# Output projection of a feed-forward block in two-by-two blocks: the pair groups as three, four and four in place of four, four and three

## What is computed

```python
def conv_ffn(x, w_in, conv_w, conv_b, w_out):        # x: 1 x 1024 x 1024
    h = causal_depthwise_conv(x @ w_in, conv_w, conv_b)  # w_in: 1024 x 5632, three taps along the tokens
    val, gate = jnp.split(h, 2, axis=-1)
    return (jax.nn.silu(gate) * val) @ w_out         # w_out: 2816 x 1024
...
x = x + conv_ffn(rms_norm(x, norm_ffn_g), ...)
```

## Time and profile before

| | |
|---|---|
| three executions | 2439.64, 2433.68, 2439.77 us; median 2439.64 |
| the profiled execution | 2434.73 us; its span 2432.9 us |
| TensorE matmul busy | 2294.0 us, 94% of the span |
| VectorE, ScalarE, GpSimd busy | 1598.2, 1293.5, 1076.4 us |
| mean granted TensorE clock | 0.982 |
| first matmul of P0, start | 1916.46 us |
| units 1 to 13 end | 2429.8 us, then the last addition and the last transfer out |

### The profile page before, as it was taken

How to read it: one execution, slowest core, us unless ns; L and a number is a source line. 1 busy time by engine, 2 the same in 40 slices (tenths; PEclk the granted TensorE clock), 3 DMA queues, 4 the chain that set the end, 5 groups by cost and what they waited for, 6 DMA issues and landing times. The chain is left out here.

```text
span 2432.9 us, 35474 instructions
## 1 busy us (share of the span) xinstructions
PE 2294.0 (94%) x11778; PEld 1940.5 (80%) x11778; DVE 1598.2 (66%) x3055; ACT 1293.5 (53%) x2966; POOL 1076.4 (44%) x1125
## 2 busy tenths in 40 slices
PE   7999999999999999999999998989988999997999
PEld 6788778878888878888888887877767788875787
DVE  7444666667885333356656665587978688897975
ACT  6444566666775434456656665555544454553432
POOL 5554322311245642321222223577766656564643
PEclk9999999999999999999999999999989999998999
DMA  6322101111243332222223224422343623345732
GB/s 220 113 71 66 40 23 31 31 33 49 64 135 100 94 128 70 91 74 83 83 85 92 85 83 144 137 86 85 96 160 109 186 87 102 102 150 187 226 108 82
DMA packets 332164, 242.73 MB, mean 100 GB/s; under 512 B 66256, under 2 KB 286672, under 8 KB 331472
## 3 DMA queue, kind: packets, MB, share of 16 engines
q1 hardware_dynamic: 331984, 240.47, 32.4%
HBM read 196.64 MB, written 43.78 MB: 99 GB/s over the span
## 5 line engine op out<-in xcount | busy, mean ns | idle before, releaser
L2758 POOL TENSOR_TENSOR WS<-WR,WS 128x256 fp32r<-128x256 f32 x647 | 505.4, 801 | 982.0 <-ACT WS L2110 979.5
L1869 PE MATMUL PS<-HT,WS 128*128 128x512 f32 x1488 | 605.2, 407 | 32.5 <-POOL WS L2758 9.4
L1871 PE MATMUL PS<-HT,WS 128*128 128x512 f32 x1488 | 586.3, 394 | 0.0
L1870 PE MATMUL PS<-HT,WS 128*128 128x512 f32 x1488 | 584.3, 393 | 0.0
L1869 PEld LDWEIGHTS PS<-HT,WS 128*128 128x128 f32 x1488 | 282.8, 190 | 94.6 <-issue 26.0
L1871 PEld LDWEIGHTS PS<-HT,WS 128*128 128x128 f32 x1488 | 282.0, 190 | 62.2
L1870 PEld LDWEIGHTS PS<-HT,WS 128*128 128x128 f32 x1488 | 283.1, 190 | 52.2
L2110 ACT ACTIVATE PT<-PS 128x512 fp32r<-128x512 f32 x352 | 186.3, 529 | 222.3 <-PE PS L1982 221.9
L2110 ACT ACTIVATE WS<-WR 128x256 fp32r<-128x256 f32 x662 | 247.2, 410 | 105.0 <-PE PS L1871 57.0
L2350 DVE TENSOR_TENSOR PT<-PS,PT 128x512 fp32r<-128x512 f32 x352 | 210.8, 609 | 66.9 <-ACT PT L2110 64.5
L2015 PE MATMUL PS<-PT,QKV 128*128 128x256 f32 (+1 forms) x1248 | 208.1, 288 | 3.4 <-DVE YB L2529 2.3
(11 more groups left out here) (297 smaller groups left out, 4922.6 us busy)
## 6 DMA issues: line engine op xcount, KB each, us to landing
WR<-in_w_in_odd SPq DMA_DIRECT2D x106, 256.0 KB, 2.9
EO<-in_grid SPq DMA_DIRECT2D x48, 384.0 KB, 3.1
WR<-in_ffn_in SPq DMA_DIRECT2D x64, 256.0 KB, 2.9
WR<-in_w_in_even SPq DMA_DIRECT2D x100, 128.0 KB, 2.5
WR<-in_w_out_odd SPq DMA_DIRECT2D x48, 256.0 KB, 2.8
yd<-PY SPq DMA_DIRECT2D x44, 256.0 KB, 3.2
WR<-ud SPq DMA_DIRECT2D x39, 256.0 KB, 3.1
EO<-in_ffn_in SPq DMA_DIRECT2D x35, 256.0 KB, 3.0
```

The lines of the kernel that those rows point to most:

```text
L1869: e.matmul(out, wh, rh, start=start, stop=False)
L1870: e.matmul(out, wh, rl, start=False, stop=False)
L1871: return e.matmul(out, wl, rh, start=False, stop=stop)
L2758: e.tensor_tensor(ws(i, 1, n), RAW[raw_slot(u)][:, o:o + n], f32(ws(i, 0, n)), ALU.subtract).then_inc(s_wlop.sem, 1)
```

## The change

```diff
-GROUPS = ((0, 4), (8, 4), (16, 3))
+GROUPS = ((0, 3), (6, 4), (14, 4))
```

## The result

| | before | after |
|---|---|---|
| median | 2436.28 us (20 runs, 2433.68 to 2440.96) | 2443.41 us (20 runs, 2437.31 to 2447.67) |
| ratio | | 1.0027 [1.0020, 1.0034] |
| profiled execution, span | 2434.73, 2432.9 us | 2438.33, 2436.5 us |
| TensorE, VectorE, GpSimd busy | 2294.0, 1598.2, 1076.4 us | 2293.9, 1599.0, 1078.6 us |

What follows compares the result with a forecast made beforehand. VectorE's work at the first group's entry, then two chained reloads, and VectorE nearly from P103 to P126 were taken as bounds. Terms -12 - 5.5 + 0.8 + 1.4 + 19.04 = +3.7 us gave 2443 us, range 2430 to 2453.

Steps and rivals of the forecast that it cites:

- up to P99's addition: Entry of the first group: fewer low parts, narrower weight sums and shorter VectorE waits bring this addition 12 us earlier.
- P103 to P126: Units 8 and 9: VectorE becomes the bound, the stretch takes 60.7 us, 5.5 less than 66.25.
- unit 10: Starts with VectorE a little further behind; its loss of 1.38 us grows to about 2.2, +0.8.
- unit 12: Loses 1.4 us because unit 11 now prepares four pairs rather than three.
- I count for each what VectorE lost to one GpSimd instruction: Entry: five of seven removed low parts ran while VectorE worked, each giving back 1.1 us, 5.5 us together.
- unit 7 near 39: Sign that the forecast holds: unit 7 takes near 39 us, where it took 47.96.
- no stop ahead of P96 over 2 us: Sign at the entry: TensorE's 6.08 us stop ahead of P96 shrinks to about 1, none over 2.
- The chain of the reloads: Entry: from reload 0's issue to P99's addition, two reload latencies one behind the other, kept at 13.3 us.
- P102's stop: Entry: TensorE still stops ahead of P102 about as long as before, 12 us.
- Rival 1: Entry healed, VectorE's lateness all gone: P99's addition 24.7 us earlier, total -9.0, 2431 us; chance 0.15.
- Rival 2: Unit 9 stuck: P103 to P126 takes its 66 us again, total +9.2, 2449 us; chance 0.2.
- Rival 3: Load ring and SyncE's strict order bind: only 6 us up to P99, total +9.7, 2449 us; chance 0.1.

Runs made afterwards that it cites:

- a1: Kernel before (groups 4,4,3) with the seven GpSimd low parts of the first group's fourth pair left out: 2431.64 us, ratio 0.9977.
- a3: Changed kernel (3,4,4) with the 21 VectorE low parts of the second group left out: 2436.31 us, ratio 1.0002 to the kernel before.
- a4: Changed kernel (3,4,4) with all 28 loads of the second group's operands left out: 2439.0 us, ratio 1.0011 to the kernel before.
- b1: Kernel before (4,4,3) with reloads of X ahead of the same product's u loads, reload 2 right behind reload 0: 2428.91 us, ratio 0.9962.
- b2: Changed kernel (3,4,4) with reloads of X ahead of u loads, reload 2 right behind reload 0: 2434.96 us, ratio 0.9991 to the kernel before.
- b3: Kernel before with groups of 4, 3 and 4 pairs in place of 4, 4, 3: 2443.27 us, ratio 1.0027.
- a2: Kernel before (4,4,3) with the seven loads of the first group's fourth pair left out: 2435.79 us, ratio 0.9996.
- b4: Kernel before (4,4,3) with the first group's fourth-pair low parts on VectorE in place of GpSimd: 2433.49 us, ratio 0.9983.
- c1: Kernel before (4,4,3) with the reloads first and the first group's fourth low parts on VectorE: 2426.21 us, ratio 0.9958.
- c2: Kernel before (4,4,3) with the reloads first and every group's fourth low parts on VectorE: 2425.05 us, ratio 0.9948.
- c3: Changed kernel (3,4,4) with the reloads first and all low parts of u on VectorE: 2432.95 us, ratio 0.9983 to the kernel before.

## Why the prediction was right or wrong

The forecast of 2443.0 against a median of 2443.41 is closer than its steps deserve: it was built on a median of before that is 3.4 us above the one of 20 runs, and the sum was 3.4 too small (+3.7 against +7.1). By its own steps, in the stage:

| term | predicted | measured |
|---|---|---|
| up to P99's addition | -12 | -9.5 |
| P103 to P126 | -5.5 | -4.7 |
| unit 10 | +0.8 | -1.4 |
| unit 12 | +1.4 | +1.4 |
| units 12 and 13 longer | +19.0 | +19.0 |
| sum | +3.7 | +4.8 |

- **What bounds it** was right: VectorE's work at the entry, the reload chain, and VectorE in P103 to P126. a1 and a3 show the first and the last; the chain's cause was seen only in part, below.
- **Up to P99's addition** is the term that failed most. It was made of 8 us of VectorE's busy time and 4 of its waits, with the chain unchanged. Measured: busy 59.35 to 54.97, so 4.4; the waits for tiles of u 5.86 to 3.22, so 2.6; the chain 2.4 shorter. The step "I count for each what VectorE lost to one GpSimd instruction" has the right price (a1: 1.1 each) and the wrong conclusion, that what is left of GpSimd's work would not come to lie on VectorE's: three instructions did, for 3.3 us. The sums were priced from one slow row (1.77), while the four took 5.86 together; they gave back 3.65 and not 1.1, and the low parts of u 0.4. For the same reason "unit 7 near 39" and "no stop ahead of P96 over 2 us" failed: 42.50 and 2.55. That the three moved is read from the traces, with a1, where they stayed, as the nearest control; no run moved them alone.
- **The chain of the reloads** was described as standing behind loads that wait for "those very splits", and then kept at 13.3. I didn't ask which loads stand there: the last two or three are those of the second group, which nobody needs yet. The 2.4 by which the chain did shrink came mostly from transfers that landed sooner, which the step didn't foresee. a4, b1 and b2 show that 6 to 7 us of the entry were there in both kernels.
- **P102's stop** as long as before (12.03), P103's shorter than the 4 foretold (2.86).
- **P103 to P126**: VectorE is 58.77 us busy (58.7 foretold) of 61.49 (60.7), 95.6%. The mechanism is right (a3), the idle time kept is 2.7 rather than 2.
- **Unit 10** was to fall further behind and instead lost nothing. What VectorE is behind is now paid inside unit 9, at P123 and P124 (a stop of 4.07), ahead of the boundary. The mechanism was right, its place wrong, and the term had the wrong sign.
- **The rivals.** Rival 1 didn't come about: P99's addition is 9.5 us earlier, not 24.7. Rival 2 foretold 66 us for P103 to P126 and has 61.5; as a general mechanism (a light unit can't use its short products) it holds for 7 of 9.5 us (b3). Rival 3 foretold 6 us up to P99 and the entry gave 9.5; the number of loads is out by a2, but the strict order of SyncE's list, which it names too, held up the reloads by some 6 us in both kernels (a4, b1, b2).
- **Still open:** the stage gives +4.8, the medians +7.1. The profiled executions differ by +3.6, of which -1.3 is the part ahead of unit 7. The trace of after is of one of its fastest executions, 5.1 under the median, that of before 1.6 under its own, so what the slower executions lose stands in neither. Over the five kernels with 3,4,4 the ratio of times exceeds what the stage shows by -0.7 to 3.2 us, so it's no steady term, and I can't place it.

## What to carry to other kernels

Moving the light part of a job to the front helps only if the engine that is late there is freed by the lightening: here matmuls went away and VectorE's additions, splits and taps stayed, so 20.5 us in units 12 and 13 were given up for 15.6 in units 7 to 10. Before resizing stages, read what stands *ahead* of the late transfer on its queue; moving two reloads past loads that could not start anyway gave 0.9962, while neither other table of groups gained anything. And when an instruction on a neighbouring engine is taken away, look where the rest of that engine's list will fall: what ran in an idle gap may come to lie where it hurts as much.

## What the hardware showed unexpectedly

A subtraction on GpSimd beside VectorE mostly cost VectorE more than doing it itself: seven low parts moved onto VectorE shortened its busy time to P103 from 59.35 to 58.32 us and the kernel by 3.9 us (b4). The same move for a later group took 2.4 us off its busy time from P103 to the end of unit 10 (c1 87.2, c2 84.9) and 2.6 off units 11 and 12 (b2 62.6, c3 60.0); once, from P103 to the end of unit 10 with 3,4,4, it added 0.6 (b2 82.4, c3 83.1). An undisturbed one takes VectorE 0.67 us; one of the seven on GpSimd takes 1.27 to 2.02 and costs VectorE 1.1 if it is at work (a1), and nothing if it stands idle. Side by side in the stretch from 2170.73 to 2179.23, each got one instruction through in 1.70 us.

Transfers of 305 GB/s, at a share of 0.93 for 29.6 us, ran beside a unit 9 that lost only 1.0 us (a3); the prediction had seen no more than 217.
